# Delta rule of a two-block model: triangular inverse taken on 32x32 diagonal blocks and finished by one off-block step, with ScalarE's rates and exponentials moved

## The reference, cut to what matters

```
cum   = cumulative log decay inside the chunk
alpha = kk * exp(-c*(cum - own)),  beta = kk*rate * exp(c*cum),  kappa = key * exp(c*cum),  rho = r * exp(-c*cum)
A     = strictly triangular part of (beta^T alpha)          64x64 in a chunk
Tinv  = (I + A)^-1                                          triangular, unit diagonal
solve = Tinv alpha^T,  Tinv (kappa alpha) v                 then the chunk's outputs and state update
S'    = decay * S + ...                                     chunk to chunk (the scan)
```

## Time and profile before

| | |
|---|---|
| median of 3 runs | 2647.64 us (2647.13 to 2650.81) |
| span of the profiled execution | 2655.0 us |
| PE busy / MATMUL records | 2489.5 us (94%) / 19578 |
| DVE, ACT, POOL busy | 1696.8, 1059.9, 418.4 us |
| the delta rule's groups g = 0, 1, 2, 3 | 605.9 to 667.1, 667.1 to 729.1, 741.0 to 801.9, 801.9 to 859.7 us |
| the two scans | 729.1 to 741.0 us, 859.7 to about 873 us |

### The profile page before, as it was taken

The page is one execution under the profiler, slowest core; times in us unless marked ns, Lnnn a source line. Parts: engine busy times, 40 slices in busy tenths (PEclk is TensorE's granted clock), DMA queues, the critical chain, the costliest instruction groups (busy, mean ns, idle before and its releaser), DMA issues.

```text
span 2655.0 us, 49488 instructions
## 1 busy us (share of the span) xinstructions
PE 2489.5 (94%) x19578; PEld 2041.4 (77%) x19578; DVE 1696.8 (64%) x2787; ACT 1059.9 (40%) x1750; POOL 418.4 (16%) x372
## 2 busy tenths in 40 slices
PE   6999999988888999999999999889999998899977
PEld 4888888757777778888788888669997875577857
DVE  2877787565554687778887754665555334565664
ACT  4222224454333542222522223455455343455344
POOL 2000001024445300000100001001013600121042
PEclk9999999989999999999999999999999999899999
DMA  7766662200000166666466652315563321023401
GB/s 264 226 194 193 195 204 94 81 5 4 4 4 12 56 195 192 193 194 201 157 205 193 194 149 89 98 51 159 181 180 104 96 91 40 1 64 123 126 14 48
DMA packets 88434, 323.55 MB, mean 122 GB/s; under 512 B 9712, under 2 KB 10864, under 8 KB 87504
## 3 DMA queue, kind: packets, MB, share of 16 engines
q1 hardware_dynamic: 86864, 310.68, 38.0%
q0 software_dynamic: 1408, 10.59, 1.1%
HBM read 320.18 MB, written 1.05 MB: 121 GB/s over the span
## 4 chain that ended last, share of the span: by engine, by line
PE 80%; DVE 9%; ACT 5%; issue 4%; DVEq 1%; DMA 1%; POOL 0%; POOLq 0%; ACTq 0%; SPq 0%
PE bank L502 21%; PE bank L504 21%; PE bank L503 21%; PE bank L2177 4%; PE bank L1389 1%; PE bank L1380 1%; DVE row_statistics L1434 1%; DVE weights_hi_lo L408 1%; PE bank L1405 1%; ACT work L1495 1%; ACT weights_hi_lo L403 1%; DMA weight_ring<-stream_k 1%; PE bank L1809 1%; ACT work L1504 1%; PE bank L2800 1%
## 5 line engine op out<-in xcount | busy, mean ns | idle before, releaser
L403 ACT ACTIVATE weights_hi_lo<-weight_ring 128x1024 fp32r<-128x1024 f32 (+1 forms) x381 | 396.7, 1042 | 1085.7 <-PE bank L504 1060.7
L408 DVE TENSOR_TENSOR weights_hi_lo<-weight_ring,weights_hi_lo 128x1024 fp32r<-128x1024 f32 (+1 forms) x374 | 454.6, 1216 | 481.4 <-ACT weights_hi_lo L403 479.7
L502 PE MATMUL bank<-input_hi,weights_hi_lo 128*128 128x512 f32 (+1 forms) x2032 | 743.8, 366 | 18.9 <-DVE input_lo L813 12.3
L503 PE MATMUL bank<-input_lo,weights_hi_lo 128*128 128x512 f32 (+1 forms) x2032 | 740.3, 364 | 0.0
L504 PE MATMUL bank<-input_hi,weights_hi_lo 128*128 128x512 f32 (+1 forms) x2032 | 740.1, 364 | 0.0
L502 PEld LDWEIGHTS bank<-input_hi,weights_hi_lo 128*128 128x128 f32 x2032 | 386.6, 190 | 85.7 <-issue 22.9
L503 PEld LDWEIGHTS bank<-input_lo,weights_hi_lo 128*128 128x128 f32 x2032 | 386.7, 190 | 60.2 <-issue 0.7
L504 PEld LDWEIGHTS bank<-input_hi,weights_hi_lo 128*128 128x128 f32 x2032 | 386.5, 190 | 59.9
L502 PE MATMUL bank<-hidden_hi_lo,weights_hi_lo 128*128 128x512 f32 (+1 forms) x952 | 343.5, 361 | 5.0 <-DVE hidden_hi_lo L1109 2.1
L504 PE MATMUL bank<-hidden_hi_lo,weights_hi_lo 128*128 128x512 f32 (+1 forms) x952 | 340.2, 357 | 0.0
L503 PE MATMUL bank<-hidden_hi_lo,weights_hi_lo 128*128 128x512 f32 (+1 forms) x952 | 340.2, 357 | 0.0
(11 more groups left out here) (515 smaller groups left out, 3110.9 us busy)
## 6 DMA issues: line engine op xcount, KB each, us to landing
weight_ring<-stream_k SPq DMA_DIRECT2D x498, 512.0 KB, 3.7
weight_ring<-stream_f SPq DMA_DIRECT2D x64, 448.0 KB, 3.4
weight_ring<-stream_f SPq DMA_DIRECT2D x32, 512.0 KB, 3.7
extra_tiles<-condrows POOLq DMA_DIRECT2D x3, 1024.0 KB, 9.3
constants<-consts POOLq DMA_DIRECT2D x1, 2112.5 KB, 9.0
residual_stream<-xin SPq DMA_DIRECT2D x1, 2048.0 KB, 12.1
work<-nabias POOLq DMA_DIRECT2D x1, 2048.0 KB, 8.9
residual_stream<-ctx POOLq DMA_DIRECT2D x1, 1024.0 KB, 6.2
```

Source lines behind the costliest of these rows:

```text
L403: act.activation(split_place(place)[:, 0, 0:words], w[:, 0:words], ACT.Copy).then_inc(hi_ready, 1)
L408: eng.tensor_tensor(split_place(place)[:, 1, 0:words], ring[:, n % RING, 0:words], split_place(place)[:, 0, 0:words].bitcast(F32), ALU.sub ...
L502: pe.matmul(out, weights[:, 0, w], x_hi, start=first, stop=False)
L503: pe.matmul(out, weights[:, 0, w], x_lo, start=False, stop=False)
```

## The change

The diagonal 32x32 blocks of A are computed, masked and inverted by levels 2, 4, 8, 16 on tiles half as wide (128x256: 8 cells of 32x32 in each of the four quarters of the partitions). Matmuls become 32x32x32: `square` issues 32 for a unit where it issued 16. `within` issues three products by 32-column blocks (near blocks both ways, and the off-diagonal block), 96 matmuls for a unit where it issued 32. The last level computes the off-diagonal block alone: `across` (16 matmuls a unit), `near_blocks` (identity and zero products that write the finished diagonal blocks and zeros into a 64x64 layout, 48 a unit), `across_turned` (16 a unit). ScalarE copies the assembled inverse into `INVERSE` (the tile of `AT`), and VectorE puts the off-diagonal block beside it with two copies.

VectorE's triangles and updates, GpSimd's masks and ScalarE's copies of X work on 256 columns instead of 512. VectorE has one copy more at the start (the off-diagonal block of A). GpSimd issues its masks first and keys and factors behind them. ScalarE makes both units' rates between the levels (behind levels 0 and 2) and both units' decays behind the copies of the solutions; VectorE's two running sums stand behind the last level. Rates get the factor tiles of their own unit. The constants shrink by 320 columns.

```diff
+SUB = 32
-          ("sel_f", 64), ("mu", 7 * P), ("ml", 7 * P), ("cu", 6 * HD), ("cl", 6 * HD), ("su", HD), ("sl", HD), ("iu", HD),
-          ("il", HD),
+          ("sel_f", 64), ("mu", 7 * P), ("ml", 7 * P), ("cu", 5 * SUB), ("cl", 5 * SUB), ("su", HD), ("sl", HD), ("iu", HD),
+          ("il", HD), ("su32", SUB), ("sl32", SUB), ("id32", SUB), ("zero32", SUB),
...
-            return (SIG1, CUM1, AA1) if n == 1 else (SIG0, CUM0, AA0)
+            if n < 2:
+                return (SIG1, CUM1, AA1) if n else (SIG0, CUM0, AA0)
+            return FACTORS[n % 2][0], FACTORS[n % 2][2], WORK[:, 8 + n % 2, :]
...
+            def near_products(b, o, x, y, beside):
+                for tt in range(TT):
+                    for k in range(4):
+                        for hb in range(2):
+                            rows, i, j = HALF[hb], tt * P + k * SUB, tt * P + (k ^ beside) * SUB
+                            mm = pe.matmul(pb[b + hb][QUARTER[k], o + tt * SUB:o + (tt + 1) * SUB], x[rows, i:i + SUB],
+                                           y[rows, j:j + SUB], start=True, stop=True)
+                return mm
+
             def within(n):
                 al, be, _ = FACTORS[n % 2]
                 pe.wait_ge(factors_ready, n + 1)
-                products(2 * (n % 2), 0, be, al)
-                products(2 * (n % 2), 1, al, be).then_inc(within_ready, 1)
+                near_products(2 * (n % 2), 0, be, al, 0)
+                near_products(2 * (n % 2), P, al, be, 0)
+                near_products(2 * (n % 2), 2 * P, be, al, 1).then_inc(within_ready, 1)
...
-            def square(bank, x, y):
+            def square(bank, x, x0, y):
                 for i in range(2 * TT):
-                    for half in HALF:
-                        o = slice(i * HD, (i + 1) * HD)
-                        mm = pe.matmul(pb[bank][half, o], x[half, o], y[half, o], start=True, stop=True)
+                    for rows in QUARTER:
+                        mm = pe.matmul(pb[bank][rows, near(i)], x[rows, x0 + i * SUB:x0 + (i + 1) * SUB], y[rows, near(i)],
+                                       start=True, stop=True)
+                return mm
+
+            def across(u):
+                for i in range(2 * TT):
+                    for k in first_rows(d):
+                        mm = pe.matmul(pb[u][QUARTER[k ^ 1], near(i)], AT[u][QUARTER[k], HALF_T + i * SUB:HALF_T + (i + 1) * SUB],
+                                       TI[u][QUARTER[k], near(i)], start=True, stop=True)
+                return mm
+
+            def near_blocks(u):
+                for i in range(2 * TT):
+                    for k, rows in enumerate(QUARTER):
+                        o = i * HD + k % 2 * SUB
+                        pe.matmul(pb[4 + u][rows, o:o + SUB], C("id32")[rows, :], TTI[u][rows, near(i)], start=True, stop=True)
+                for i in range(2 * TT):
+                    for k in first_rows(1 - d):
+                        o = i * HD + (1 - k % 2) * SUB
+                        mm = pe.matmul(pb[4 + u][QUARTER[k], o:o + SUB], C("id32")[QUARTER[k], :], C("zero32")[QUARTER[k], :],
+                                       start=True, stop=True)
+                return mm
+
+            def across_turned(u):
+                for i in range(2 * TT):
+                    for k in first_rows(d):
+                        mm = pe.matmul(pb[u][QUARTER[k], near(i)], XS[u][QUARTER[k ^ 1], near(i)],
+                                       TTI[u][QUARTER[k ^ 1], near(i)], start=True, stop=True)
                 return mm
...
+                    if li < LAST:
+                        pe.wait_ge(level_masked, NIN * g + 2 * li + u + 1)
+                        square(u, MB[u], li % 2 * HALF_T, TI[u]).then_inc(x_ready, 1)
+                    else:
+                        across(u).then_inc(x_ready, 1)
...
+                if li == LAST:
+                    for u in range(2):
+                        pe.wait_ge(t_updated, turned_update(g, li - 1, u) - 2 * g)
+                        near_blocks(u).then_inc(z_ready, 1)
...
                     if li < LAST:
-                        square(2 + u, TTI[u], XS[u])
-                    square(4 + u, XS[u], TTI[u]).then_inc(z_ready, 1)
+                        square(2 + u, TTI[u], 0, XS[u]).then_inc(z_ready, 1)
+                        square(4 + u, XS[u], 0, TTI[u]).then_inc(z_ready, 1)
+                    else:
+                        across_turned(u).then_inc(z_ready, 1)
...
-                        act.activation(XS[u], pb[u][:, :], ACT.Copy).then_inc(x_copied, 1)
-                    if g == 3 and li < 4:
+                        act.activation(XS[u][:, 0:HALF_T], pb[u][:, 0:HALF_T], ACT.Copy, scale=1.0 if li < LAST else -1.0)\
+                            .then_inc(x_copied, 1)
+                    if g < 3 and li in (0, 2):
+                        wkv_rates_scalar(act, 2 * g + 2 + li // 2)
...
-                    if g < 3 and li == 0:
-                        wkv_rates_scalar(act, 2 * g + 2)
-                    if g < 3 and li == 2:
-                        wkv_decays_scalar(act, 2 * g + 2)
-                    if g < 3 and li == 4:
-                        wkv_rates_scalar(act, 2 * g + 3)
+                for u in range(2):
+                    act.wait_ge(z_ready, near_read(g, u))
+                    act.activation(INVERSE[u], pb[4 + u][:, :], ACT.Copy).then_inc(factors_by_token, 1)
...
                 if g < 3:
+                    wkv_decays_scalar(act, 2 * g + 2)
                     wkv_decays_scalar(act, 2 * g + 3)
...
+                    else:
+                        dve.wait_ge(z_ready, across_read(g, u))
+                        dve.wait_ge(factors_by_token, NTOK * g + 6 + u + 1)
+                        for k in first_rows(d):
+                            beside = INVERSE[u][QUARTER[k], :].rearrange("p (i h c) -> p i h c", h=2, c=SUB)[:, :, 1 - k % 2, :]
+                            ins = dve.tensor_copy(beside, tiles(pb[u][QUARTER[k], 0:HALF_T], SUB))
+                        ins.then_inc(t_updated, 1)
             if g < 3:
-                wkv_decay_sums(dve, 2 * g + 3)
+                for n in (2 * g + 2, 2 * g + 3):
+                    wkv_decay_sums(dve, n)
```

More of the change, by code:

```diff
@@ L2021, in build @@
         LAST = len(BLOCK_LEVELS) - 1
+        NIN = 2 * LAST
+        NUPD = 4 * LAST + 4
+        NTOK = 8
+        QUARTER = [slice(SUB * k, SUB * k + SUB) for k in range(4)]
+        HALF_T = 2 * TT * SUB
         CORNERS = [(0, 0), (1, 1), (0, 1), (1, 0)]
@@ L2043, in by_half, with near, near_cells, near_bank_pair @@
             return ap.rearrange("p (t h c) -> p h t c", h=2, c=HD)
+        def near(i):
+            return slice(i * SUB, (i + 1) * SUB)
+        def near_cells(ap):
+            return ap[:, 0:HALF_T].rearrange("p (h t c) -> p h t c", h=2, c=SUB)
+        def near_bank_pair(b, o):
+            return banks[:, b:b + 2, o:o + TT * SUB].rearrange("p h (t c) -> p h t c", c=SUB)
+        def plain_update(g, li, u):
+            return NUPD * g + 4 * li + 2 * u + 1
+        def turned_update(g, li, u):
+            return NUPD * g + 4 * li + 2 * u + 2
+        def near_read(g, u):
+            return NUPD * g + 4 * LAST + u + 1
+        def across_read(g, u):
+            return NUPD * g + 4 * LAST + 2 + u + 1
+        def across_added(g, u):
+            return (NUPD - 2) * g + 4 * LAST + u + 1
+        def first_rows(d):
+            return (0, 2) if d == 0 else (1, 3)
         def bank_pair(b, q):
@@ L2207, in wkv_ends_tensor @@
                         for half in HALF:
-                            pe.matmul(pb[2 + 4 * u][half, cell(hb, tt)], TTI[u][half, cell(hb, tt)],
+                            pe.matmul(pb[2 + 4 * u][half, cell(hb, tt)], INVERSE[u][half, cell(hb, tt)],
                                       TOKA[u][half, chunk(tt, hb)], start=True, stop=True)
@@ L2212, in wkv_ends_tensor @@
                         for half in HALF:
-                            mm = pe.matmul(pb[3 + 4 * u][half, cell(hb, tt)], TTI[u][half, cell(hb, tt)],
+                            mm = pe.matmul(pb[3 + 4 * u][half, cell(hb, tt)], INVERSE[u][half, cell(hb, tt)],
                                            KV[u][half, cell(hb, tt)], start=True, stop=True)
@@ L2261, in wkv_rates_scalar @@
             if n >= 2:
[L2262 removed]
+                act.wait_ge(factors_ready, n - 1)
             act.activation(sig, pb[w][:, :], ACT.Sigmoid, bias=V("w0", n))
@@ L2331, in wkv_gpsimd @@
             for g in range(4):
-                n0 = 2 * g + 2
-                masks(g, 0)
-                masks(g, 1)
+                for li in range(LAST):
+                    masks(g, li)
                 if g < 3:
[L2336 to L2346, removed]
+                    for n in (2 * g + 2, 2 * g + 3):
+                        wkv_keys(pool, n)
+                    for n in (2 * g + 2, 2 * g + 3):
+                        wkv_factors(pool, n)
+                        if g != 1:
```

(19 more changed lines are left out.)

55 lines of the change are left out of this document (32 added, 23 removed).

## The result

The changed kernel takes 2773.02 us (2771.44 to 2782.01, 4 runs) against 2648.62 us (median of 4 runs); the ratio is 1.0478 (95% interval 1.0456 to 1.0499), +124 us, 4.8% slower. The forecast was 2756 us, in a range of 2724 to 2802.

A forecast was written before the change was run, and what follows sets the result against it. It took TensorE's code supply in the delta rule as the bound: +99.7 us for packets and +8 for the clock, +108 on a profiled 2655.0 gives 2763, less 7.4 from span to median, 2756 us; range 2724 to 2802.

The forecast's parts named there:

- Instruction count: TensorE in the delta rule: a group goes from 1828 to 3044 records and from 14.3 to 23.8 code packets.
- Code supply binds, one packet ahead: TensorE's delta rule waits for code packets of 128 matmul records, only one fetched ahead: +99.7 us; chance 0.74.
- The share f of at most 0.08: Part of a code block executed before the next fetch begins; halved record time shortens the period by under 0.1 us.
- Record price of 7.3 to 14.7 ns: TensorE's own time per 32x32 record, 0.9 to 1.9 us a packet, under 3.4 us, so costing nothing.
- The work beside TensorE, at nothing: Halved copies, updates and masks, moved decays and running sums, fewer table loads: all covered by TensorE's time, costed at nothing.
- 99.7 + 8: Extra time in the four delta-rule groups: +99.7 us for code supply and +8 us for the clock.
- the packet's period: Time per code packet on TensorE when code is short: 3.59 us, bounds 3.4 to 3.73 us.
- the clock term: Stalls lower TensorE's clock in solves, key values and low ranks: 2 us a group, +8; bounds 0 and 39 in all.
- the step from span to median: Whole kernel: the median of the runs lies 7.4 us below the profiled span, taking 2763 to 2756 us.
- The second: Delta rule: code supply binds and long stalls keep TensorE at 1.2 GHz, 2787 us; chance 0.14.
- the first: Delta rule: code supply binds and the clock mostly holds, 2756 us; chance 0.74.
- The third and fourth: Code comes in time: faster, 2608 us, chance 0.05; or no record starts within 14.7 ns of another, 2671, chance 0.04.

The follow-up runs named there:

- split_columns: Kernel before with each 64x64x64 matmul of its square cut into two streaming 32 columns each: 2740.09 us, ratio 1.0342.
- scalar_move: Kernel before with only the change's moves of rates, exponentials, running sums and GpSimd's order, inverse left on 64x64 cells: 2649.86 us, ratio 1.0011.
- double_columns: Changed kernel with each 32x32 matmul of its square streaming 64 columns instead of 32, same instructions and result: 2762.19 us, ratio 1.0430.
- half_records: Changed kernel with each matmul of its square covering two neighbouring cells, half the instructions, same columns, some values wrong: 2680.95 us, ratio 1.0126.

## Why the prediction was right, and where it was off

- **Instruction count.** 3044 records and 23.8 packets a group: the totals are 24442 records and 155 packets, against 24440 and 155 forecast.
- **Code supply binds, one packet ahead.** Shown from three sides, supported by a fourth: idle "issue" time grew by some 100 us with nothing else to wait for; taking records away gave 26 to 30 ns a record where a record takes 15; adding columns cost nothing; and, less firmly, saving records by merging gave 19 us here and 7 in a kernel short of code only at its group ends. Not shown: that the waits are for the packet and not for another step of decoding. The packets and the gaps have the same period and the same count, and that is all the trace has.
- **The share f of at most 0.08.** Its argument took 29.2 ns as a record's own price, which fits `split_columns`, and the shorter records did not shorten the period: in the chain above it is 3.8 us, in the earlier trace rows 3.73.
- **Record price of 7.3 to 14.7 ns.** The chain has 15 ns at a clock of 0.50 (127 records in 1.93 us), just over the bound worked out for full clock. It cost nothing: even twice and three times the columns fitted.
- **The work beside TensorE, at nothing.** `scalar_move`: 0 to 6 us. In the levels TensorE waited for neither VectorE nor ScalarE.
- **The terms that were too small.** 99.7 + 8 was forecast, 124.5 came in the groups, 16.8 us more. Both the packet's period and the clock term were too small. The period: 3.59 us was taken, and 14.6 packets of the levels took 57.8, 57.0, 54.1 and 52.1 us in the four groups, 3.97, 3.91, 3.71 and 3.58 us each. That is 12 us above the forecast for the levels; the values of g=0 and g=1 lie above both rows that the period was taken from. Why it was longer there stays open: the clock was 0.56 to 0.58 in all four, so the clock alone doesn't set it, and yet in `double_columns`, at 0.87 to 0.95, all four were within 1.4 us of the forecast, 14.6 x 3.59 = 52.3. The clock: I took a fifth of its bound, from one sparse stretch in 242 us, and it stood at its lower level for most of the levels. What that cost beside the period is seen in g=1 in the solves, 5.00 us against 3.70, and in the low ranks behind level 2, 3.71 us against 1.91. Starts and ends together took 145 us in the four groups where 132 were forecast without the clock term, and 145 in `double_columns` too. How the 13 us divide between the clock and the code no run separates.
- **What else is in the total.** The forecast for the profiled execution was 2763 us and 2769.6 came. That looks closer than it was: the stretches outside the groups, which the change hardly touches, were 9.9 us shorter. Against that, 7.4 us were taken off for the step from span to median, as it stood in one profiled execution before, and now the median is 3.4 us above the span. The two nearly cancel by chance, so the 17 us by which the total missed are those of the groups.
- **The rivals.** The second (clock at the lower level) was half true: 0.65 to 0.72 over the groups. The measured 2773 lies about midway between its 2787 and the 2756 of the first. The third and fourth, code in time, are excluded by the "issue" time and by `half_records`.

## What to carry to other kernels

Count the instructions before the arithmetic. Halving a tile doubles the instructions for the same columns, and the unrolled code of small matmuls had a supply rate of its own here, 256 instructions in 3.45 to 4 us; look for evenly spaced "issue" gaps and code packets in the profile, and see which stretches stand just above that rate. Where they do, merge matmuls that share weights; and don't alternate tile sizes inside a stretch. Look at the granted clock too: it was lower in these stretches, and solves and low ranks paid for it.

## What the runs showed of the hardware beside that

- A 64x64 fp32 record on two corners costs 29.2 ns with 64 streamed columns and 29.3 ns with 32, so streaming 64 columns instead of 32 cost nothing there (clock 1.00).
- Alternating 32x32 and 64x64 weights costs 0.59 us a pair at the lower clock level, against 4 records x 52 ns = 0.21 us with one size.
- The granted clock was 0.69 over the groups of the changed kernel, and 0.88 when the same instructions streamed 64 columns instead of 32. In a stretch at 0.50 TensorE ran 127 records in 1.93 us and then waited 1.9 us, again and again.
